# Two input blocks by seven block products with their operand sums made by adding transfers, and the last cross-attention output product in two halves with the router's root on ScalarE

## The reference, cut to what matters

```
h = RMSNorm(x); P = h @ W_in                      # 2048 x 3136, nine column groups
o = concat[window attention | conv | latent attention | state space]; x = x + o @ W_out
x = x + CrossAttn(RMSNorm(x), RMSNorm(mem))       # ends in  o @ xa_wo, 512 x 2048
h = RMSNorm(x); g = h @ w_group; e = h @ w_expert # 4 groups, 8 experts in each
top-1 group, top-2 experts in it, softmax gates
x = x + sum over experts of gate * ((silu(h @ w_gate) * (h @ w_up)) @ w_down)   # 32 experts
```

## Time and profile before

| | |
|---|---|
| median of 3 runs | 1413.32 us (1412.78 to 1415.44) |
| the profiled execution | 1413.58 us, its span 1411.8 us |
| PE busy | 1210.6 us (86%) |
| DVE busy | 593.1 us (42%) |
| ACT busy | 208.4 us (15%) |
| POOL busy | 13.9 us (1%) |
| DMA | 477.79 MB, mean 338 GB/s; queue 1: 61392 packets, queue 0 (POOL's): 864 packets |

### The profile page before, as it was taken

The page is one execution under the profiler, slowest core; times in us unless marked ns, Lnnn a source line. Parts: engine busy times, 40 slices in busy tenths (PEclk is TensorE's granted clock), DMA queues, the critical chain, the costliest instruction groups (busy, mean ns, idle before and its releaser), DMA issues.

```text
span 1411.8 us, 16085 instructions
## 1 busy us (share of the span) xinstructions
PE 1210.6 (86%) x6731; PEld 566.3 (40%) x6731; DVE 593.1 (42%) x1222; ACT 208.4 (15%) x461; POOL 13.9 (1%) x31
## 2 busy tenths in 40 slices
PE   8999999999999999887667978777878687787777
PEld 4785565656885632322222222222322222222223
DVE  5999984858754442331122322222222222222222
ACT  3311023351022411100000000000001000000001
POOL 3000000000000000000000000000000000000000
PEclk9999999999999999998888988888889878988898
DMA  9343454333556879999999999999999999999998
GB/s 288 140 150 132 155 190 169 130 120 138 180 239 233 308 312 431 432 431 434 429 431 431 430 431 428 433 431 431 430 431 432 431 431 430 430 431 430 431 424 318
DMA packets 62728, 477.79 MB, mean 338 GB/s; under 512 B 13701, under 2 KB 21253, under 8 KB 45504
## 3 DMA queue, kind: packets, MB, share of 16 engines
q1 hardware_dynamic: 61392, 476.40, 81.8%
q0 software_dynamic: 864, 0.25, 0.3%
q10 hardware_dynamic: 400, 0.10, 0.0%
HBM read 474.63 MB, written 2.11 MB: 338 GB/s over the span
## 4 chain that ended last, share of the span: by engine, by line
PE 58%; DMA 36%; DVE 3%; ACT 2%; issue 1%; SPq 1%; DVEq 0%; ACTq 0%
DMA ring<-in_moe_w_up_dram 20%; DMA late_ring<-in_moe_w_up_dram 14%; PE bank L1294 11%; PE bank L733 10%; PE bank L1329 7%; PE bank L748 5%; PE bank L1050 5%; PE bank L1315 2%; PE bank L717 2%; PE bank L1253 2%; PE bank L1174 2%; PE bank L798 2%; PE bank L1130 2%; PE bank L1019 2%; DMA ring<-in_moe_w_down_dram 1%; PE bank L1366 1%
## 5 line engine op out<-in xcount | busy, mean ns | idle before, releaser
L1294 PE MATMUL bank<-ring,x_gathered 128*32 128x512 f32 x1184 | 252.2, 680 | 52.0 <-DMA late_ring<-in_moe_w_up_dram 36.0
L1294 PE MATMUL bank<-late_ring,x_gathered 128*32 128x512 f32 x800 | 202.3, 682 | 38.8 <-DMA ring<-in_moe_w_up_dram 37.4
L2760 DVE TENSOR_TENSOR tokens_out<-tokens_out,bank 128x512 f32<-128x512 f32 x240 | 148.5, 680 | 202.6 <-PE bank L1366 202.6
L2743 DVE SCALAR_TENSOR_TENSOR hidden<-hidden,bank 128x128 f32<-128x128 f32 x31 | 8.9, 287 | 338.8 <-ACT hidden L1898 338.8
L733 PE MATMUL bank<-ring,hT 128*128 128x512 f32 (+2 forms) x384 | 142.1, 530 | 0.1
L1294 PEld LDWEIGHTS bank<-ring,x_gathered 128*32 128x32 f32 x1184 | 67.0, 123 | 142.2 <-issue 137.5
L1253 PE MATMUL bank<-x_tok,select 128*32 128x512 f32 x512 | 115.9, 1032 | 7.3 <-DVE select L2652 4.2
L1329 PE MATMUL bank<-ring,hidden 128*32 128x512 f32 x560 | 89.1, 793 | 18.2 <-DVE hidden L2745 18.2
L733 PEld LDWEIGHTS bank<-ring,hT 128*128 128x128 f32 x384 | 72.7, 190 | 66.9 <-issue 59.6
L1294 PEld LDWEIGHTS bank<-late_ring,x_gathered 128*32 128x32 f32 x800 | 53.3, 123 | 111.4 <-issue 108.9
L1366 PE MATMUL bank<-y_slots,weight_slots 32*128 32x512 f32 x496 | 72.0, 651 | 28.8 <-ACT y_slots L1913 21.0
(11 more groups left out here) (472 smaller groups left out, 1235.0 us busy)
## 6 DMA issues: line engine op xcount, KB each, us to landing
ring<-in_moe_w_up_dram SPq DMA_DIRECT2D x19, 4096.0 KB, 40.3
ring<-in_moe_w_down_dram SPq DMA_DIRECT2D x16, 4096.0 KB, 29.6
ring<-in_moe_w_gate_dram SPq DMA_DIRECT2D x16, 4096.0 KB, 38.9
late_ring<-in_moe_w_down_dram SPq DMA_DIRECT2D x13, 4096.0 KB, 29.6
late_ring<-in_moe_w_gate_dram SPq DMA_DIRECT2D x12, 4096.0 KB, 39.6
late_ring<-in_moe_w_up_dram SPq DMA_DIRECT2D x10, 4096.0 KB, 38.1
ring<-in_w_in_dram SPq DMA_DIRECT2D x20, 1024.0 KB, 8.1
ring<-in_w_out_dram SPq DMA_DIRECT2D x16, 1024.0 KB, 6.5
```

The costliest lines, as they stand in the source:

```text
L1294: mm = pe.matmul(gu_bank[SLOTS * c:SLOTS * c + SLOTS, :], XGT[:, at, n % 4, n // 4, :], pieces[c % 2][:, FF * (n % 8):FF * (n % 8) + FF], ...
L2760: ins = v.tensor_tensor(y, x, mix[c][:, :], ALU.add)
```

## The change

**Order.** The pieces and the banks come in a new order: `ckv`, `skv`, `y1`, then `cq`, `sq`, then all eight memory tiles. `mem_ln_g` gets a tile of its own, since `GB` now holds a sum.

**Seven products.** For `cq` and `sq` the product of [256 tokens, 2048] and [2048, 512] is cut into 2 x 2 x 2 blocks (two token tiles, two halves of the 16 chunks, two halves of the columns) and made with seven products of 8 matmuls of 256 columns. Besides the blocks themselves they need four sums of blocks of `HT` (T1 to T4, [128, 8, 128], 0.5 MB, one set for both groups) and four sums of weight blocks in each group (S1 to S4, [128, 8, 256], 1 MB). ACT writes one operand, copied or negated, and POOL then issues a transfer that adds the other operand onto it (`accum_op=ALU.add`), from `HT` for T1 to T4 and from the weights in DRAM for S1 to S4. ACT counts its parts in `parts_ready`; `SUMMED` says which semaphore and count stands for which sum. Three old semaphores are shared, so POOL also waits where a second transfer on one semaphore must not overlap the first. ACT drains the four banks of a group (`drain_seven`), and `join_seven` on DVE adds them up in five instructions ahead of the norms.

**Last product and root.** `co31` becomes two banks of 256 columns, each with its own residual, squares and turned blocks. DVE drains the first pair of turned blocks, ACT the second. ACT takes the square root (its table is loaded by a dummy instruction after `group_exps(0)`), DVE the reciprocal and one correction step. The filler products around it are cut from 2 + 5 to 0 + 3.

The diff, cut to its core:

```diff
-    t += ["zg1", "cq0", "cq1", "ckv0", "ckv1", "sq0", "sq1", "skv0", "skv1"]
-    t += [f"mT0{q}" for q in range(4)] + ["y1"] + [f"mT1{q}" for q in range(4)]
+    t += ["zg1", "ckv0", "ckv1", "skv0", "skv1", "y1"] + [f"{g}{part}" for g in ("cq", "sq") for part in "cbad"]
+    t += [f"mT{tt}{q}" for tt in range(TT) for q in range(4)]
...
+        T8 = [scr[:, a:a + 1024].rearrange("p (k t) -> p k t", k=8) for a in (10240, 8192, 11264, 9216)]
+        S8 = {"cq": [eights(GB[:, :]), eights(scr[:, 0:2048])], "sq": [eights(scr[:, 2048:4096]), eights(GB[:, :])]}
+        JOIN = {"cq": (CQ, flat(URB)), "sq": (SQ[:, :, :], flat(SQT[:, :, :]))}
...
-                    if g in ("za", "sq") and q < 2:
+                    if g in ("za", "skv") and q < 2:
                         sp.wait_ge(s["half_used"], 1 if g == "za" else 2)
+                    elif g in ("cq", "sq") and q < 2:
+                        wait_filled(sp, g + "c")
...
+            def accumulate(ready, dst, src, name):
+                pool.wait_ge(s["parts_ready"], ready)
+                pool.dma_start(dst, src, accum_op=ALU.add).then_inc(s[SUMMED[name][0]], 16)
...
+            accumulate(1, t1, hT8(1, 1), "T1")
+            accumulate(2, c1, block8_source("cq", 0, 1), "cqS1")
+            accumulate(3, t3, hT8(0, 0), "T3")
+            wait_sum(pool, "cqS1")
+            accumulate(4, block8("cq", 0, 1), block8_source("cq", 1, 1), "cqS3")
+            accumulate(5, t2, hT8(0, 0), "T2")
+            wait_sum(pool, "cqS3")
+            accumulate(6, c2, block8_source("cq", 1, 1), "cqS2")
+            accumulate(7, t4, hT8(1, 0), "T4")
+            wait_sum(pool, "T3")
+            accumulate(8, q1, block8_source("sq", 0, 1), "sqS1")
+            accumulate(9, block8("cq", 1, 0), block8_source("cq", 1, 0), "cqS4")
+            wait_sum(pool, "T4")
+            accumulate(10, block8("sq", 0, 1), block8_source("sq", 1, 1), "sqS3")
+            accumulate(11, q2, block8_source("sq", 1, 1), "sqS2")
+            accumulate(12, block8("sq", 1, 0), block8_source("sq", 1, 0), "sqS4")
...
+            def seven(g):
+                by8(a[:, 0:T], hT8(0, 0), block8(g, 0, 0))          # after pieces 0, 1
+                by8(b[:, 0:T], hT8(1, 0), block8(g, 1, 0)).then_inc(s["half_used"], 1)   # pieces 2, 3
+                by8(d[:, T:2 * T], t3, block8(g, 0, 1))             # T3, S3
+                filled(by8(c[:, 0:T], t1, s1))                      # T1, S1
+                filled(by8(b[:, T:2 * T], t4, block8(g, 1, 1)))     # T4
+                filled(by8(a[:, T:2 * T], t2, s2))                  # T2, S2
+                filled(by8(d[:, 0:T], hT8(1, 1), block8(g, 1, 0)))  # S4
...
+            act.wait_ge(s["scan_done"], 5)
+            part(t1, hT8(0, 1), 1.0)
+            pieces_arrived("cq", 0)
+            part(c1, block8("cq", 0, 0), -1.0)
+            part(t3, hT8(0, 1), -1.0)
+            part(block8("cq", 0, 1), block8("cq", 0, 1), -1.0)      # then the drains of skv
+            act.wait_ge(s["scan_done"], 8)
+            wait_sum(act, "T1")
+            part(t2, t1, -1.0)
+            drain("y1", OT[:, 14:16, :], four(2))
+            wait_sum(act, "cqS1")
+            part(c2, c1, -1.0)
+            wait_sum(act, "T2")
+            part(t4, t2, 1.0)
+            pieces_arrived("sq", 0)
+            part(q1, block8("sq", 0, 0), -1.0)
+            wait_sum(act, "cqS2")
+            act.wait_ge(s["half_used"], 3)
+            part(block8("cq", 1, 0), c2, -1.0)
+            part(block8("sq", 0, 1), block8("sq", 0, 1), -1.0)
+            wait_filled(act, "cqc")
+            wait_sum(act, "sqS1")
+            part(q2, q1, -1.0)
+            drain_seven("cq")
+            wait_sum(act, "sqS2")
+            act.wait_ge(s["half_used"], 4)
+            part(block8("sq", 1, 0), q2, -1.0)
+            drain_seven("sq")
...
-            wait_task(dve, "ckv1")
+            join_seven("cq")        # 5 instructions: 256, 256, 256, 512, 512 elements a row
-            wait_task(dve, "skv1")
+            join_seven("sq")
...
-            cross_out(1, 3)
+            last_out_half(0)
+            last_out_half(1)
+            turn_eighth(0)
             route_quarter(1, 2)
-            turn_quarter(1, 3)
-            keep_warm("pos1", 2)
-            route_quarter(1, 3)
+            turn_eighth(1)
+            route_last()
...
+                    dve.wait_ge(s["root"], TT + 1)
+                    link(v.reciprocal(y, SM[:, 286:287]))
+                    link(v.tensor_scalar(w, y, y, a, ALU.mult, ALU.mult))
+                    link(v.scalar_tensor_tensor(y, w, -3.0, y, ALU.add, ALU.mult))
+                    link(v.tensor_scalar(RS[:, 1:2], y, -0.5, None, ALU.mult))
```

More of the change, by code:

```diff
@@ L134, in task_order @@
           "xp10", "xp11", "rl0"]
-    t += ["xo1", "co01", "pos0", "co11", "hT10", "co21", "hT11", "hT12", "co31", "hT13", "rl1"]
+    t += ["xo1", "co01", "pos0", "co11", "hT10", "co21", "hT11", "hT12", "co31a", "co31b", "hT13a", "hT13b", "rl1"]
     t += ["pos1", "cnt", "tab"]
@@ L149, in piece_order @@
 def piece_order():
-    w = [(g, q) for g in ("u", "za", "zg", "cq", "ckv", "sq", "skv") for q in range(4)]
+    w = [(g, q) for g in ("u", "za", "zg", "ckv", "skv", "cq", "sq") for q in range(4)]
     w += [("xv", q) for q in range(4)]
@@ L160 @@
 PIECES = piece_order()
-LAST_USE = {"u": "u1", "za": "za1", "zg": "zg1", "cq": "cq1", "ckv": "ckv1", "sq": "sq1", "skv": "skv1",
+LAST_USE = {"u": "u1", "za": "za1", "zg": "zg1", "cq": "cqd", "ckv": "ckv1", "sq": "sqd", "skv": "skv1",
             "wqb": "mq11", "wkvb": "mkv11", "xv": "xv1", "glu": "glu1", "xk": "xk1", "pw": "pw1", "wo0": "wo01",
@@ L281, in trunk @@
         GM = sb("mix_gain_cols", [P, KD], stack=front)
+        MG = sb("memory_gain_cols", [P, KD], stack=front)
         BL = sb("ssm_b_lhs", [P, 2, 4, P], stack=front)
@@ L734, in token_major @@
                                    start=i == 0, stop=i == n - 1)
-                    if name == "sq1" and i == 7:
+                    if name == "skv1" and i == 7:
                         mm.then_inc(s["half_used"], 1)
@@ L1688, in _ @@
             drain_memory(0)
-            drain("y1", OT[:, 14:16, :], four(2))
             drain_memory(1)
@@ L1870, in _ @@
             group_exps(0)
+            st.link(nc.scalar.activation(SM[:, 287:288], const("eps"), ACT.Sqrt))
             skip("co21")
@@ L1875, in _ @@
             drain_turned(1, 2)
-            skip("co31")
-            quarter_square(1, 3)
-            drain_turned(1, 3)
+            skip("co31a", "co31b", "hT13a")
+            for h in range(2):
+                wait_task(act, f"co31{'ab'[h]}")
+                st.link(nc.scalar.activation(XGS[:, 0:T], X[:, 1, 1536 + T * h:1536 + T * h + T], ACT.Square,
+                                             scale=float(D) ** -0.5, accum_out=SM[:, 283 + h:284 + h]), "m_sq")
+            act.wait_ge(s["mean_part"], TT + 1)
+            st.link(nc.scalar.activation(SM[:, 286:287], SM[:, 284:285], ACT.Sqrt, scale=1.0, bias=SM[:, 285:286]), "root")
+            wait_turn(act, "hT13b")
+            drain("hT13b", HT[:, 14:16, P:T], four(2), cols=T)
+            st.link(nc.scalar.activation(SM[:, 287:288], const("eps"), ACT.Exp))
             skip("rl1", "pos1")
```

146 lines of the change are left out of this document (122 added, 24 removed).

## The result

The changed kernel takes 1449.16 us (median of 4 runs, 1446.31 to 1454.07), the kernel before 1413.38 on the same chip: a ratio of 1.0252, interval 1.0239 to 1.0266. That is 35.8 us slower; forecast were 13.1 us and a range that ended at 1434. The profiled execution took 1454.07 us, span 1452.3, at the upper end of those runs.

A forecast was written before the change was run, and what follows sets the result against it. PE was taken to bound the front, and DMA's stream of expert weights the last 900 us. Additions + 13.8, xv0's wait + 1.0 and the router's part - 1.8 gave + 13.0 on 1413.6, so 1426.5; range 1407.5 to 1434.

The forecast's parts named there:

- The products: PE's cq and sq: seven products of eight take 24.2 us, saving 3.3 in each group, 6.6 in both.
- The adding transfers: Sums for cq and sq: chained transfers land late, making the end of sq 13.8 us later than before.
- timeline with doubled reads: cq and sq sums if each byte written needs two read: sq ends at 214.6, 17.7 us later than before.
- just in time: sq's sums: they land as its products need them, so sq takes 24.2 us more after cq, to 214.6.
- The three quarters: Price of additions: three quarters of the way from copy (2.1 later) to doubled read (17.7 later), giving 13.8.
- `xv0`'s wait: After sq, xv0 waits for ACT's drains while PE turns memory tiles: 1.0 us lost.
- DVE's cap: conv_sq on DVE stays at 224.8, so the seven-products part can never give more than 5.2 us.
- The router's part: Last output product and root: the logits' scale ends 1.8 us earlier after co31, bounds 0.8 to 2.2.
- The sums come in time: Rival for the chained sums: below about 7.0 us per transfer the change is faster, 1407 to 1410.5; chance 0.28.
- An addition costs what a copy costs: Rival for the adding transfers: + 2.1 + 1.0 - 1.8 = 1414.9, between 1411 and 1417; chance 0.17.
- POOL is the bound: Rival: POOL takes 5 us to write each 1024-row adding transfer, 60 us for twelve, 1436 or more; chance 0.05.

The follow-up runs named there:

- light_loads: Changed kernel with the loads of blocks sq and xv and of MLA's query projection cut to 16 elements per partition, every addition kept: 1432.94 us (1.0136).
- probe: Separate kernel computing nothing of the reference, issuing single transfers of the change's shapes: a lone 1 MB addition took 9.11 us.
- pool_sums: Changed kernel with all twelve sums made by GpSimd arithmetic in SBUF, no adding transfers or ACT passes, front constants on their own semaphore: 1453.45 us (1.0284).
- tiny: Changed kernel with each adding transfer cut to a copy of 16 elements per partition, sums missing, parts, products, waits and joins kept: 1410.65 us (0.9981).
- copies: Changed kernel with each of the twelve adding transfers replaced by a plain copy of the same bytes, same queue and waits: 1427.96 us (1.0101).
- sq_seven: Changed kernel with seven products in sq alone, cq back to two accumulations, eight additions left, front constants on their own semaphore: 1434.08 us (1.0148).
- s3_own: Changed kernel with cq's S3 on its own semaphore, so POOL no longer waits for S1 before S3, nor S3 before S2: 1449.85 us (1.0258).

## Why the prediction was right in sign and wrong in size

- **The products.** Right: eight in a row took 27.91 us in `light_loads`, so seven take 24.4, and 24.2 was forecast. But the first of the seven was forecast at 142.0 and came at 145.69. Of this, 2.6 go with the front constants' semaphore, shared with a later load in the change: DVE and PE waited for both (at most 1.0 us), and in this execution PE ran at the lower clock behind it. That wait stands in the diff and I did not cost it. With the semaphores apart the start is 142.89.
- **The adding transfers: this step failed.** The term of 13.8 us was mis-sized. It is net of the 6.6 us that the products save (190.3 is the end without waits, 196.9 the old one), so it stands for 20.4 us of loss by the additions; measured are 38.5 between no additions and all of them. In the profiled execution the end of `sq` is at 237.1, which is 22.5 us behind the timeline with doubled reads (214.6), and the forecast took 3.9 off that timeline. Link by link, issue to landing in us:

| `cq` | timeline with doubled reads | changed kernel | `light_loads` |
|---|---|---|---|
| S1 | 12 | 15.6 | 10.7 |
| S3 | 9.4 | 9.5 | 9.1 |
| S2 | 7.9 | 9.7 | 9.5 |
| S4 | 15.7 | 18.7 | 13.2 |
| issue of S1 to landing of S4 | 47 | 56.3 | 45.3 |

- Where the 22.5 us come from:
  - The chain of `cq` took 9.3 us longer (56.3 against 47). The timeline had put the loads at the right links, S1 and S4, but let an addition and a load share the engines evenly; in the probe an addition landed with the last of the four loads beside it (17.6). And a lone addition was priced at 7.9 where it takes 9.11; the 5.3 us of engine time for one more was right.
  - The chain began 4.8 us late: S1 was issued at 144.77, not at 140.
  - `sq`'s sums were put "just in time" without a timeline of their own. From 176.79 to 231.6 they took 54.9 us and held PE for 4.11 more; the chain that ended last runs through them.
  - The clock was no term of the sum. The slower records behind the last two waits add 4.0 us (12.68 - 10.52 and 5.41 - 3.62). The four come to 22.2.
- **The three quarters** were taken on the argument that the operand in SBUF need not share every limit. The lone additions within SBUF (4.53 against 2.90) show no such discount. The Trainium skill's figure for it, doubled reads, in "Collectives: The Full Stack", section "The bandwidth ceiling: the fold count and why AG ≠ RS ≠ AR", measured there on reductions between cores, would have given 16.6, an estimate; the 5.3 us of a queued addition, against 2.6 for a loaded MB, agree with it.
- **A case of luck.** In `light_loads` the end of `sq` is at 215.8, next to the timeline's 214.6. That does not make the timeline right: it had the shares of `sq`'s loads in it, which are gone in that run, and a lone addition too cheap, and the two errors about cancel.
- **`xv0`'s wait** on the drains: 1.30 before it, as forecast (1.0). **DVE's cap** never came into play: PE was later than DVE in every run but `pool_sums`, where DVE was the bound.
- **The router's part.** Its direction was right, 1.36 against 1.8: the last product of the router now ends behind ACT's root, and the logits wait 0.32 us for it.
- **The rivals.** "The sums come in time" is refuted by `tiny` against the changed kernel. "An addition costs what a copy costs" is refuted twice: the additions cost 21 us more than copies, and the copies 13 us more than that case gave. "POOL is the bound": its issue was 1.55 us for 1024 rows, not 0.54, but the 18.7 us of issue in all lay almost wholly under the landings.

That the loads and the additions could be interleaved so that the loss vanishes isn't excluded by these runs; one attempt failed. Additions with other row sizes were not tried in this kernel; alone, 8 KB rows took 7.95 us for the MB in place of 9.11. Nor was the new order without seven products, so what the order by itself costs or gives is not shown.

## What to carry to other kernels

An adding transfer on a chain is priced link by link, by what runs beside each: here 9.5 us with no load under way and 15 to 19 beside loads of 1 MB. The loads beside it are late too: in `copies` and `sq_seven` PE waited for one of them. A scheme that trades PE time for DMA time needs its operands well ahead, or it trades 3.3 us of products for three landings in a row. And where PE waits 4 us or more, as here, the slower records behind the last wait (1.8 to 2.2 us for each) belong in the sum.

## What the runs showed of the hardware

- An addition of 1 MB into SBUF: 9.11 us alone (a copy on the same queue 6.26, a load by SP 5.40), 5.3 more for one queued behind it, 17.6 beside four 1 MB loads (`probe`, one execution).
- GpSimd adds two [128, 2048] tiles in 4.5 us and holds up DVE's instructions on tiles in SBUF meanwhile (`pool_sums`: one tap up to 4.76 us in place of 0.48).
- One semaphore counted by two loads makes the user of the first wait for the second: at most 1.0 us in the front. In three of eight profiles with the shared semaphore PE's clock was at 0.57 to 0.59 in 96 to 100 us behind it, which cost 1.7 us more; in the other five, and in all with the semaphores apart, it was 1.00. What brings the dip is open.
- These kernels spread more than the one before (1442.75 to 1451.42 for `s3_own`, 1413.19 to 1415.08 for the kernel before beside it).
